# Output projections: four evictions first, the rest of each new tile of x as steps inside the next group

## The reference, cut to what matters

```python
def rmsnorm(x, g):
    xf = x.astype(jnp.float32)
    y = xf * lax.rsqrt(jnp.mean(xf * xf, axis=-1, keepdims=True) + EPS) * g.astype(jnp.float32)
    return y.astype(x.dtype)
...
        x = x + jnp.concatenate([ya, yb], axis=-1) @ w_out[l]
    return rmsnorm(x, final_norm_g)
...
    return x + merged @ w_out.astype(x.dtype)
```

## Time and profile before

| | us |
|---|---|
| median of 3 runs | 2956.63 |
| lowest and highest | 2955.93, 2957.34 |
| span of the profiled execution | 2956.8 |

### The profile page before, as it was taken

The page is one execution under the profiler, slowest core; times in us unless marked ns, Lnnn a source line. Parts: engine busy times, 40 slices in busy tenths (PEclk is TensorE's granted clock), DMA queues, the critical chain, the costliest instruction groups (busy, mean ns, idle before and its releaser), DMA issues.

```text
span 2956.8 us, 33732 instructions
## 1 busy us (share of the span) xinstructions
PE 2841.3 (96%) x13276; PEld 2324.0 (79%) x13276; DVE 1342.4 (45%) x1855; ACT 999.1 (34%) x1558; POOL 1092.7 (37%) x536
## 2 busy tenths in 40 slices
PE   7999999999999999999999999999999999999985
PEld 5888887778888888777777888788878888888774
DVE  6656545732365555474135445444344222222345
ACT  5234434522323343452333233323223232333221
POOL 3443341234443333222434333333434444444431
PEclk9999998999999999899999999999999999999997
DMA  5332231234433223113433222222323333336332
GB/s 158 105 102 72 72 113 37 55 100 139 139 93 121 72 68 117 42 42 96 137 123 85 72 72 75 75 72 68 97 86 112 110 114 107 114 107 214 110 111 93
DMA packets 307613, 288.11 MB, mean 97 GB/s; under 512 B 33152, under 2 KB 256000, under 8 KB 306944
## 3 DMA queue, kind: packets, MB, share of 16 engines
q1 hardware_dynamic: 300656, 263.93, 30.0%
q10 hardware_dynamic: 6800, 22.02, 1.9%
HBM read 259.66 MB, written 26.21 MB: 97 GB/s over the span
## 4 chain that ended last, share of the span: by engine, by line
PE 80%; DVE 13%; ACT 4%; issue 2%; POOL 1%; DMA 0%; DVEq 0%; SPq 0%; ACTq 0%
PE bank L813 23%; PE bank L815 22%; PE bank L814 22%; PE work L813 2%; DVE probs L1533 2%; PE work L814 1%; PE work L815 1%; PE o_bank L813 1%; PE work L1034 1%; PE o_bank L814 1%; PE o_bank L815 1%; DVE pt L1541 1%; DVE mixed L1109 1%; DVE mixed L1108 1%; POOL w_lo L804 1%
## 5 line engine op out<-in xcount | busy, mean ns | idle before, releaser
L804 POOL TENSOR_TENSOR w_lo<-w_raw,w_hi 128x1024 fp32r<-128x1024 f32 (+3 forms) x468 | 1004.0, 2148 | 1545.0 <-ACT w_hi L669 1544.8
L813 PE MATMUL bank<-act_in,w_hi 128*128 128x512 f32 x2664 | 1058.4, 397 | 38.4 <-DVEq L1194 24.7
L815 PE MATMUL bank<-act_in,w_lo 128*128 128x512 f32 x2664 | 1044.1, 392 | 0.0
L814 PE MATMUL bank<-act_in,w_hi 128*128 128x512 f32 x2664 | 1042.7, 391 | 0.0
L669 ACT ACTIVATE w_hi<-w_raw 128x1024 fp32r<-128x1024 f32 (+3 forms) x468 | 437.8, 937 | 1096.8 <-PE bank L815 700.3
L813 PEld LDWEIGHTS bank<-act_in,w_hi 128*128 128x128 f32 x2664 | 503.3, 189 | 149.4 <-POOL w_lo L804 18.3
L815 PEld LDWEIGHTS bank<-act_in,w_lo 128*128 128x128 f32 x2664 | 502.3, 189 | 108.2
L814 PEld LDWEIGHTS bank<-act_in,w_hi 128*128 128x128 f32 x2664 | 503.5, 189 | 99.3 <-issue 1.4
L813 PE MATMUL bank<-mixed,w_hi 128*128 128x512 f32 x768 | 303.0, 394 | 6.4 <-POOL w_lo L804 6.4
L814 PE MATMUL bank<-mixed,w_hi 128*128 128x512 f32 x768 | 301.7, 393 | 0.0
L815 PE MATMUL bank<-mixed,w_lo 128*128 128x512 f32 x768 | 301.0, 392 | 0.0
(11 more groups left out here) (230 smaller groups left out, 2897.7 us busy)
## 6 DMA issues: line engine op xcount, KB each, us to landing
w_raw<-in_w_in SPq DMA_DIRECT2D x512, 128.0 KB, 2.4
w_raw<-in_w_in SPq DMA_DIRECT2D x224, 256.0 KB, 2.9
w_raw<-in_w_out SPq DMA_DIRECT2D x64, 512.0 KB, 3.6
w_raw<-in_w_in SPq DMA_DIRECT2D x32, 512.0 KB, 3.7
w_raw<-in_w_out SPq DMA_DIRECT2D x64, 256.0 KB, 4.7
probs<-in_xT SPq DMA_DIRECT2D x32, 256.0 KB, 4.8
x_scr<-buf ACTq DMA_DIRECT2D x32, 256.0 KB, 2.2
probs<-x_scr SPq DMA_DIRECT2D x32, 256.0 KB, 4.9
```

Source lines behind the costliest of these rows:

```text
L804: nc.gpsimd.tensor_tensor(lo, raw, hi, ALU.subtract).then_inc(lo_ready, 1)
L813: pe.matmul(dst, lhs[0], rhs[0], start=start, stop=False, skip_group_check=skip)
L814: pe.matmul(dst, lhs[0], rhs[1], start=False, stop=False, skip_group_check=skip)
L815: return pe.matmul(dst, lhs[1], rhs[0], start=False, stop=stop, skip_group_check=skip)
```

## The change

The second loop of `evac_x`, and the squares of layer 2, become four steps `x_rest` of their own, one for each tile, and ACT's four calls of `new_x_hi` go with them. They are placed 1, 3, 5 and 7 products into the next group (behind the last group of all, at once). In layer 2 all four scalings of the old x stand ahead of the first eviction. The waits for x_saved move behind the scalings.

```diff
-        rank = {"values": 1, "hi": 2, "output": 2, "read": 3, "mla_norm": 4, "gate_log": 5}.get(step[0], 0)
+        rank = {"values": 1, "hi": 2, "output": 2, "read": 3, "mla_norm": 4, "gate_log": 5, "x_rest": 6}.get(step[0], 0)
...
             steps.append(("evac", n))
+        if kind == "wo":
+            for mm in range(4):
+                if n < len(groups) - 1:
+                    later(2 * mm + 1, "x_rest", n, mm)
+                else:
+                    steps.append(("x_rest", n, mm))
...
-                    elif kind == "wo":
-                        for m in range(4):
-                            new_x_hi(l, 4 * i + m, xk[0])
-                            xk[0] += 1
+                elif name == "x_rest":
+                    g = groups[step[1]]
+                    new_x_hi(g["l"], 4 * g["i"] + step[2], xk[0])
+                    xk[0] += 1
...
                 for mm in range(4):
                     m, k = 4 * i + mm, KT * (l + 1) + 4 * i + mm
-                    kx = k - KT
                     v.wait_ge(x_landed[m % 4], 16 * (k // 4 + 1))
+                    if l == 2:
+
+                        res = x_slot(m)
+                        ins = v.scalar_tensor_tensor(res, res, gains[:, G_FINAL1 + m:G_FINAL1 + m + 1], acc2[:, :],
+                                                     ALU.mult, ALU.mult)
+                if l == 2:
+                    link(ins)
+                for mm in range(4):
+                    m, kx = 4 * i + mm, KT * l + 4 * i + mm
                     if l < 2 and kx >= 4:
                         v.wait_ge(x_saved[m % 4], 16 * (kx // 4))
                     elif l == 2 and i == 0:
                         v.wait_ge(x_saved[m % 4], 16 * (2 * KT // 4))
-                    res = x_slot(m)
-                    if l == 2:
-
-                        link(v.scalar_tensor_tensor(res, res, gains[:, G_FINAL1 + m:G_FINAL1 + m + 1], acc2[:, :],
-                                                    ALU.mult, ALU.mult))
                     full(gi, mm)
-                    v.tensor_tensor(buf[:, mm, :], bank[mm][:, :], res, ALU.add).then_inc(x_new, 1)
+                    v.tensor_tensor(buf[:, mm, :], bank[mm][:, :], x_slot(m), ALU.add).then_inc(x_new, 1)
                     v.wait_ge(x_new, kx + 1)
                     signal(bank_free)
                     signal(x_read)
-                    if l == 2 and mm > 0:
-                        add_square(m == 1, acc[:, :], sq_count(k - 1))
+
+            def x_rest(gi, mm):
+
+                l, i = groups[gi]["l"], groups[gi]["i"]
+                m, k = 4 * i + mm, KT * (l + 1) + 4 * i + mm
+                if l < 2:
+                    link(lo_of_x(l, m, buf[:, mm, :], k))
+                    add_square(m == 0, acc[:, :], sq_count(k))
+                elif i < 3:
+
+                    link(split(mixed[:, m], buf[:, mm, :]))
+                if l == 1:
+                    add_square(m == 0, acc2[:, :], sq_count(k) + 1)
                 if l == 2:
-                    add_square(False, acc[:, :], sq_count(k))
-                for mm in range(4):
-                    m, k = 4 * i + mm, KT * (l + 1) + 4 * i + mm
-                    if l < 2:
-                        link(lo_of_x(l, m, buf[:, mm, :], k))
-                        add_square(m == 0, acc[:, :], sq_count(k))
-                    elif i < 3:
-
-                        link(split(mixed[:, m], buf[:, mm, :]))
-                    if l == 1:
-                        add_square(m == 0, acc2[:, :], sq_count(k) + 1)
-                    signal(tile_ready)
+                    add_square(m == 0, acc[:, :], sq_count(k))
+                signal(tile_ready)
...
+                elif name == "x_rest":
+                    x_rest(*step[1:])
```

## The result

| | median us | lowest and highest | runs |
|---|---|---|---|
| before | 2956.28 | 2954.42, 2957.34 | 4 |
| changed | 2929.47 | 2928.22, 2930.86 | 4 |

The ratio is 0.9905, 95% interval 0.9891 to 0.9919: faster, by 24 to 32 us. The forecast, 2932.6, had the sign and the mechanism, but not quite the size. Carried over by the ratio to the 2956.63 us it started from, the changed kernel takes 2928.5 us, half a us under the range of 2929 to 2941. The ends of the interval, carried over the same way, are 2924.4 and 2932.7 us.

The account below looks back on a forecast made before the run. PE, busy 96% of the span, was taken as the bound, losing time at six seams of layers 1 and 2. 12.16 + 13.09 - 1.0 - 0.2 = 24.05 us, so 2956.63 became 2932.6 us, range 2929 to 2941.

Parts of the forecast that it names:

- The bound and layer 1: PE, busy 96% of the span, bounds the kernel; removing layer 1's waits for POOL and low clock gains 12.16 us.
- T: A wo group's end, taken as the start of ACT's weight step there; the predicted times count from it.
- Weight step c+4: Layer 1, ACT's weight step after tiles 0 and 1: POOL begins at T + 9.8, 4 us of cover.
- step c+5: Layer 1, ACT's weight step after tiles 2 and 3: reached at T + 17.3, POOL done at T + 20.9.
- rival 1: Tile 2 at the seam into layer 2: DVE comes before POOL, last add 1.34 us earlier, 2931.6 us; 5%.
- the thin cover of 0.8 us: Layer 1: POOL finishes step c+5 at T + 20.9, PE needs it at T + 21.7.
- rival 3: Layer 1: step c+5 comes late if DVE is held once more beside POOL, costing 2.5 to 7.5 us; 8%.
- Layer 2: Adds of squares and scalings leave the space between evictions, so PE's bank waits go: gain 13.09 us.
- rival 5: Layer 2: scalings ahead of all evictions become the bound and make the kernel slower, 2960.7 us at d = 9.5; 3%.
- Into layer 2: First norm sum of layer 2 waits for a later last add of squares: loss 1.0 us, bounds 0 and 2.7.
- rival 2: Seam into layer 2: the clock falls at the new wait, price 1.7 us, 2934.3 us; 8%.
- The end: Last group: four adds, 1.53 us apart, stand behind the fourth eviction: loss 0.2 us, bounds 0 and 0.6.

Follow-up runs that it names:

- The scaling experiment: Changed kernel, but in layer 2 each scaling stands between the evictions again, while the adds of squares stay in the x_rest steps: 2933.84 us.
- e3_adds_between: Changed kernel, but in layer 2 the adds of squares stand between evictions again, unspread, scalings still ahead of all evictions: 2938.97 us.

## Why the prediction was right and wrong

**The bound and layer 1: right, to a tenth.** The seams vanish at all six pitches ("seven" in the prediction is a slip), and the times worked out behind T hold one by one. The timeline of the changed kernel behind the second group of layer 1 (T = 1429.48): ACT's weight steps, DVE's two held steps, POOL:

```profile
1438.14 1.05 ACT L675 ACTIVATE w_hi<-w_raw 128x1024 fp32r<-128x1024 f32 x1
1446.78 2.00 ACT L675 ACTIVATE w_hi<-w_raw 128x1024 fp32r<-128x1024 f32 x2
...
1431.19 2.38 DVE L1159 SCALAR_TENSOR_TENSOR act_in<-buf,gains,act_in 128x512 fp32r<-128x512 f32 x1 [1.00 <-ACT act_in L687]
1439.84 2.38 DVE L1159 SCALAR_TENSOR_TENSOR act_in<-buf,gains,act_in 128x512 fp32r<-128x512 f32 x1 [0.80 <-ACT act_in L687]
...
1430.62 2.40 POOL L810 TENSOR_TENSOR w_lo<-w_raw,w_hi 128x1024 fp32r<-128x1024 f32 x1 [2.17 <-ACT w_hi L675]
1439.27 2.40 POOL L810 TENSOR_TENSOR w_lo<-w_raw,w_hi 128x1024 fp32r<-128x1024 f32 x1 [6.24 <-ACT w_hi L675]
1447.91 4.76 POOL L810 TENSOR_TENSOR w_lo<-w_raw,w_hi 128x1024 fp32r<-128x1024 f32 x2 [6.24 <-ACT w_hi L675]
```

Weight step c+4 at T + 8.66 (said 8.66), POOL at T + 9.79 (9.8), step c+5 at T + 17.30 (17.3). Tile 2 is held beside POOL for the same 2.38 us as tile 0, with POOL 0.57 us ahead (said 0.58), so rival 1 did not come, and the thin cover of 0.8 us was enough, so rival 3 did not either. By the rule of the Trainium skill (SBUF — State Buffer, "Who interferes with whom") the first comer keeps the other out. Both held rows agree: POOL came first by 0.57 us, and DVE's step ends 0.55 us behind POOL's.

**Layer 2: right in size, half right in cause.** 13.12 us against 13.09. The prediction blamed the adds, and counted the scalings only as something that must not come too late. The scaling experiment shows that they were a cause of their own: 3.8 us of the pitches, where two of three were held beside POOL at every seam, and 1.1 at the end, where POOL does nothing and each takes its plain 0.75 us. I saw held scalings up to 1.78 us and did not carry them into the old order, and so expected nothing from that experiment. Ahead of the evictions the scalings were no bound, so rival 5 did not come: they ended 6.2 us before the first eviction at 2754.73.

```profile
2745.59 2.93 DVE L1170 SCALAR_TENSOR_TENSOR probs<-probs,gains,acc 128x512 f32<-128x512 f32 x4 [23.80 <-DMA probs<-x_scr]
```

**Into layer 2: mis-sized.** Said 1.0, found 1.69 in the profile pair and 1.4 in the repeats. The step that failed: PE was taken to come to its sum at 1552.09, but a sum is two matmuls, and that row is the second; PE's sum had begun 0.43 us earlier. The kernel before, then the changed one:

```profile
1551.66 1.02 PE L821 MATMUL work<-acc,ones 128*128 128x512 f32 x2
...
1534.91 1.13 PE L827 MATMUL work<-acc,ones 128*128 128x512 f32 x2 [1.14 <-DVEq L1204]
```

Counted from the last group's first eviction, the last add ends when the prediction said (22.23 us, said 22.27), the first sum starts 1.30 us later than before (22.43 against 21.13), where 1.0 was read, and the second 1.40 (24.43 against 23.03). The rest of the 1.69 in the profile pair stays open. The clock did not fall at the two waits (PEclk 1.00 from 1533 to 1545 us), so rival 2 did not come.

**The end: mis-sized.** Said +0.2, found -0.05. Four rounds stand behind the last eviction as said, but a round in the changed kernel is 1.45 us, not 1.53; that the missing signals make the difference is likely and not shown.

```profile
2890.20 0.69 DVE L1153 TENSOR_TENSOR acc<-acc,sq 128x512 f32<-128x512 f32 x1 [0.25 <-DVE buf L1181]
2891.65 0.69 DVE L1153 TENSOR_TENSOR acc<-acc,sq 128x512 f32<-128x512 f32 x1 [0.75 <-ACT sq L691]
```

**The base and the range: the step that put the forecast out of its range.** The terms of the sum are not what failed: the edited stretches gave 23.6 to 23.9 us against the 24.05 worked out. What failed is the step from that sum to a time and a range. "The profiled span lies 0.2 us above the median" was read as if span and median were the same thing. Where both are given for one execution, the time is 1.6 to 1.8 us longer than the span (2928.94 and 2927.3; 2958.88 and 2957.2). So the profiled execution before took some 2958.5 us, 2.8 over the median of the 70 runs, and the 2956.63 of three runs was itself 0.9 high. That alone moves the forecast and the time carried over to the same base alike. The low side of the range did the rest: it was the forecast's own terms and put at nothing how far runs differ in what no edit touches, though that spreads single runs of the kernel before over 12 us. Four runs against four came out 28.1 us apart by the ratio, 70 against 13 by 25.9. With 25.9 the time from 2956.63 would be 2930.7, inside the range; so that it fell half a us outside is in part the chance of few runs.

What differs is mostly the clock in the stretches ahead. They took 638.1 to 643.8 us to layer 0's first eviction, over kernels of either kind, with 47.8 us at the 1.2 GHz level in the fastest and 61.4 in the slowest; and two executions of changed kernels had 747.7 and 747.8 instead of 744 us to layer 1's. That changed programs always run the first stretch faster, as the first six profiles looked, is refuted by 639.72 under the kernel before and 643.62 under a changed one. That they do so on average is not: three profiles of the kernel before have a mean of 641.6 us, eleven of changed kernels 639.6.

Of the 25.9 us over all runs, the edited stretches make 23.6 to 23.9. In one of three profiles of the kernel before, low clock in a seam of layer 2 added 2.8 us, which the change removes with the wait; on the average of the three that is 0.9. The last us or so stays open: it may be chance, the first stretch, or low clock in layer 2 more often than three profiles show.

## What to carry to other kernels

A step that writes results back and also prepares the next stage should be cut at the point where the bank comes free: what frees the bank goes first, the rest can wait, and where it waits on an engine that also feeds the weights, it is spread so that no weight step stands behind all of it. (The spreading was worth 12 us in layer 1 and nothing in layer 2.) Moving work behind a group's end moves it towards the next fixed point, here a norm sum, which may have to move by as much; and at the very end, where no group follows, the same move is worth nothing. Before a sum is made against one profile, its stretches that the change can't touch should be held against a second profile of the same kernel.

## What was not expected of the hardware

The same idle time does not always bring the same clock. In the kernel before, PE idle for 3.06 us at a seam of layer 2 was followed by 6.83 us at 0.50, the 1.2 GHz level (the seam's second wait, 0.74 us, fell into it), in one execution and by none in two others. Of the nine seams of layer 2 in the three profiles, with waits of 2.80 to 3.07 us, this was the only one. In layer 1, shorter waits of 1.8 to 2.3 us were followed by 3.41 us at 0.50 at all nine (PEclk 0.96 over its pitches); with waits of 2.0 to 2.3 us in `e3_adds_between`, it was two of three seams of layer 2. So here the length of the wait does not tell whether the clock falls, and a wait's price is its length plus 0 or more. What decides it stays open, and so does how much of the kernel's spread from run to run (2950 to 2962 us over 70 runs before, 2928 to 2933 over 13 after) comes from it.
